# GpSimd subtracts the upper part of each output weight row block in four pieces of 256 columns, not in one of 1024

## The chip, the cores and the metric

The kernel runs on one core of a Trainium2 chip. Its time is the device time of one execution, in microseconds (us). A core has a tensor engine (PE, with its weight loads shown apart as PEld), a vector engine (VectorE, DVE in the profile), a scalar engine (ScalarE, ACT), GpSimd (POOL) and SyncE (SP), which here only issues DMAs. Each engine executes its own instructions in order; between engines there are semaphores.

## The reference, cut to what matters

One encoder layer over two sets of 512 tokens (D = 1024). The weights of interest are those of the output projection after the attention:

```python
hn = rms_norm(x, p['norm_attn'])
proj = jnp.einsum('bsd,de->bse', hn, p['w_in'])
...
oa = block_attention(qa, ka, va, 1.0 / math.sqrt(GQA_HEAD_DIM))   # 8 query heads, 2 key heads
...
ob = block_attention(qm, km, vb, 1.0 / math.sqrt(MLA_NOPE + MLA_ROPE))   # 8 heads over latents
o = jnp.concatenate([rms_norm(oa, p['out_norm_a']), rms_norm(ob, p['out_norm_b'])], axis=-1)
x = x + jnp.einsum('bse,ed->bsd', o, p['w_o'])
h2 = rms_norm(x, p['norm_ffn'])
x = x + expert_choice_moe(h2, p['w_router'], p['w_gate'], p['w_up'], p['w_down'])   # 16 experts
```

## The kernel before, in words

Matrix products of float32 are made of float32r products: each operand is split into an upper part (the value rounded to float32r) and the rest, and a product is the sum of two or three partial products. The output weights `w_o` (1024 x 1024) are split in the same way into `wo["hi"]` and `wo["lo"]`, during the attention, long before the output projection reads them.

The program goes through projection (to about 165 us), attention (to about 354 us), output projection and routing (to about 490 us), and the experts. Attention runs over 32 heads, g = 0 to 31: set 0 with its 8 GQA heads and 8 latent (MLA) heads, then set 1 likewise. Each head is four units of 128 queries. For a unit PE makes scores, VectorE takes the row maxima (`nmax`, L1471), ScalarE the exponentials (`prob`, L1403), PE turns them over (L1309), VectorE or ScalarE copies them back (`probT`), and once a head PE multiplies with the values (L1324). PE keeps three banks of scores and so runs three units ahead at most.

The order of the work is written out by hand on each engine. What touches the change:

- **GpSimd**, in each head g: the copy of the rotary keys if g starts an MLA group (`copy_rotary_keys`, L1239, for g = 24 and 25 in set 1; PE's scores of head 25 wait for the first pair), then one split of the output weights if g is in `split_at` (heads 20, 21, 22, 23, then 25, 26, 28, 29), then `add_halves(g - 2)` (L1185 and L1187), and in odd heads `scale_heads` (L1194), which multiplies two finished heads by the reciprocals of their sums.
- **A split** of row block i: `wo["hi"] = w` rounded (L1224), a wait for that, `wo["lo"] = w - wo["hi"]` (L1226), and a wait until that has ended. ScalarE has scaled the block before (L1388), one head ahead.
- **SyncE's queue**, in order: after `scale_heads(n)` it stores that pair of heads (L1136), loads two more row blocks of `w_o` (L1144, 1 MB, twice more during set 1), and loads the queries of the next two MLA heads as `q_blocks` (L1130, three DMAs for a head).
- **VectorE** turns a head's `q_blocks` over into `q_turned` (L1462), one unit before they are due. ScalarE rounds them to `qhi` (L1380), VectorE takes the rest `qlo = q_turned * gain - qhi` (L1454), a scalar_tensor_tensor with two inputs in SBUF, and PE's scores of that head wait for `qlo`. For the GQA heads the same operation reads PSUM and one tile in SBUF.

Of the kernel before, what the change touches and what calls it, by code (L numbers as in the profile page):

```python
# [13 lines left out]
F32 = mybir.dt.float32  # L14
F32R = mybir.dt.float32r
U32 = mybir.dt.uint32
ALU = mybir.AluOpType
# [7 lines left out]
SETS, SEQ, D = 2, 512, 1024  # L25
# [63 lines left out]
class Phase:  # L89
# [8 lines left out]
    def sem(self, name):  # L98
        self.sems.append(self.nc.alloc_semaphore(f"{name}_{self.suffix}"))
        return self.sems[-1]  # L100
# [912 lines left out]
def attend(phase, project_signals, a, k, att, wo, ps, banks, o_dram, r_dram, q_dram, wo_loaded):  # L1013
# [56 lines left out]
    wo_hi, wo_lo, wo_scaled = sem("wo_hi"), sem("wo_lo"), sem("wo_scaled")  # L1070
# [103 lines left out]
    def gpsimd_program(pool, row_roots, last_squares, query_roots, key_roots, row_norms, rotate_keys_pe, rotate_queries, rotate_keys, mla_parts, group_sums, acc_done):  # L1174
        LAST = T - 1

        def add_halves(g):

            n = g // 2
            rows, other = (slice(0, VD), slice(VD, P)) if g % 2 == 0 else (slice(VD, P), slice(0, VD))  # L1180
            both, head = att["ot"][g % 2][:].rearrange("d (i t) -> d i t", i=TS), att["heads"][n % OUT_RING][rows]
            pool.wait_ge(ot_copied, g + 1)
            if n >= OUT_RING:
                pool.wait_ge(o_stored[n % OUT_RING], STORED + 16 * (n // OUT_RING))
            pool.tensor_copy(head, both[other]).then_inc(o_shifted, 1)  # L1185
            pool.wait_ge(o_shifted, g + 1)
            pool.tensor_tensor(head, head, both[rows], ALU.add).then_inc(o_added, 1)  # L1187
            pool.wait_ge(o_added, g + 1)

        def scale_heads(n):  # L1190

            heads = att["heads"][n % OUT_RING]
            pool.wait_ge(r_loaded[n % 2], MLA_STORED + 32 * (n // 2 + 1))
            pool.tensor_tensor(heads, heads, att["r"][n % 2][:].rearrange("d (t i) -> d i t", i=TS), ALU.mult).then_inc(o_scaled, 1)  # L1194
            pool.wait_ge(o_scaled, n + 1)

        def finish_rows():


            row_squares, query_squares, key_squares = last_squares  # L1200
            row_squares()
            query_squares()
            pool.wait_ge(rows_ready, LAST)
            for part in mla_parts(LAST - 1):
                part()
            key_squares()
            row_roots(LAST)
            row_norms(LAST)
            rotate_keys_pe(LAST)
            rotate_queries(LAST)  # L1210
            rotate_keys(LAST)
            add_halves(0)
            query_roots(LAST)
            key_roots(LAST)
            pool.wait_ge(rk_done, T)
            add_halves(1)
            for part in mla_parts(LAST):
                part()

        def split_output_weights(pool, i):  # L1220

            raw = wo["raw"][:, i % 4, :]
            pool.wait_ge(wo_scaled, i + 1)
            pool.tensor_copy(wo["hi"][:, i, :], raw).then_inc(wo_hi, 1)  # L1224
            pool.wait_ge(wo_hi, i + 1)
            pool.tensor_tensor(wo["lo"][:, i, :], raw, wo["hi"][:, i, :].bitcast(F32), ALU.subtract).then_inc(wo_lo, 1)  # L1226

        split_at = {HEADS + 4: 0, HEADS + 5: 1, HEADS + 6: 2, HEADS + 7: 3, HEADS + QH + 1: 4, HEADS + QH + 2: 5,
                    HEADS + QH + 4: 6, HEADS + QH + 5: 7}
        copies = {QH: (2, 0, 0), QH + 1: (1, TS * QH, 2),  # L1230
                  HEADS + QH: (2, TS * (HEADS - 2), 4), HEADS + QH + 1: (1, TS * (HEADS + QH), 6)}

        def copy_rotary_keys(g):
            to, unused, count = copies[g]
            pool.wait_ge(prep_lo, prep_index["k", g // HEADS * HEADS + QH] + 1)
            if unused:
                pool.wait_ge(score_ready, unused)
            for m, part in enumerate((khi, klo)):
                pool.tensor_copy(part[to][NOPE:QK, :], part[0][NOPE:QK, :].bitcast(F32)).then_inc(pe_copied, 1)  # L1239
                pool.wait_ge(pe_copied, count + m + 1)  # L1240

        pool.wait_ge(proj_done, T)
        finish_rows()
        for g in range(GROUP, ALL):
            if g in copies:
                copy_rotary_keys(g)
            if g in split_at:
                split_output_weights(pool, split_at[g])
                pool.wait_ge(wo_lo, split_at[g] + 1)
            add_halves(g - 2)  # L1250
            if g % 2 and g > GROUP:
                scale_heads(g // 2 - 2)
        add_halves(ALL - 2)
        scale_heads(HEAD_PAIRS - 2)
        group_sums(0)
        pool.wait_ge(acc_done, 1)
        add_halves(ALL - 1)
        scale_heads(HEAD_PAIRS - 1)
# [171 lines left out]
    def vector_program(dve, row_stats, query_stats, key_stats, rb_done, rk_done, o_low, route_rest):  # L1430
# [37 lines left out]
        for u in range(NU + STEPS):  # L1468
# [30 lines left out]
            elif u == NU + 2:  # L1499
# [5 lines left out]
                      "ones_ready": ones_ready, "o_stored": o_stored, "mla_stored": project_signals["mla_stored"],  # L1505
                      "w_loaded": project_signals["w_loaded"]}
    return (sync_program, gpsimd_program, tensor_program, scalar_program, vector_program), attend_signals


# [1041 lines left out]
```

## Time and profile before

| | |
|---|---|
| median of three runs | 1035.9 us (1035.71 to 1036.63) |
| the profiled execution | 1035.18 us |
| its span, first to last instruction | 1033.4 us |
| PE busy | 1004.9 us, 97% of the span |
| VectorE busy | 850.3 us, 82% |
| ScalarE busy | 760.2 us, 74% |
| GpSimd busy | 486.2 us, 47% |
| the eight subtractions of L1226 | 19.1 us |

The shares are means over the whole program, whose stages have different limits. What matters for the change is the stretch from 270 to 340 us, where the eight splits lie, and there the order of the instructions on each engine with the idle time before them.

### The profile page before, as it was taken

The numbers are of one execution on the slowest core, as the hardware profiler recorded it, in microseconds if no ns is written. First come the engines' busy times: TensorE is split into PE (matmuls) and PEld (weight loads), VectorE is DVE, ScalarE is ACT, GpSimd is POOL, SyncE is SP. The second block draws the span as 40 slices with busy tenths as digits, with TensorE's granted clock in tenths as the row PEclk, the third lists the DMA queues.
The fourth block names the chain that finished last, engine by engine and source line by source line (L and its number), as shares of the span: only waits on it lengthen the run. The fifth ranks groups of instructions, "written<-read, shape, count | busy, mean of one in ns | idle before, by whom it ended". The sixth has DMA issues, their size and how long they took to land.

```text
span 1033.4 us, 15654 instructions
## 1 busy us (share of the span) xinstructions
PE 1004.9 (97%) x5055; PEld 806.6 (78%) x5055; DVE 850.3 (82%) x1062; ACT 760.2 (74%) x1022; POOL 486.2 (47%) x425
## 2 busy tenths in 40 slices
PE   8999999999999999995999999999999999999997
PEld 7999986666666688774888888888888888888885
DVE  6788778887888533379999999999999999999982
ACT  7665668888989745546777787778877888788772
POOL 2477679634688655446343244424442344324011
PEclk9999999999999999997999999999999999999999
DMA  9344250432443498853999999999999999999983
GB/s 330 79 116 128 79 161 12 129 72 58 129 125 71 132 254 237 232 159 142 393 398 403 398 406 411 403 400 398 420 400 402 398 419 399 403 398 408 414 330 41
DMA packets 109134, 276.02 MB, mean 267 GB/s; under 512 B 58322, under 2 KB 66733, under 8 KB 85405
## 3 DMA queue, kind: packets, MB, share of 16 engines
q1 hardware_dynamic: 103280, 258.11, 67.3%
q0 software_dynamic: 5744, 17.29, 6.7%
q8 instruction: 25, 0.41, 0.2%
q14 instruction: 25, 0.20, 0.1%
q10 hardware_dynamic: 60, 0.01, 0.0%
HBM read 247.46 MB, written 27.92 MB: 266 GB/s over the span
## 4 chain that ended last, share of the span: by engine, by line
PE 51%; DMA 1%; DVE 1%; issue 0%; ACT 0%; POOLq 0%; POOL 0%
PE ps L2223 11%; PE ps L2225 11%; PE ps L2224 11%; PE ps L2239 5%; PE ps L2237 5%; PE ps L2238 5%; PE ps L2190 1%; DMA out<-y,give 1%; DMA xt<-h,idxT 0%; DVE idx L1972 0%; DVE affT L1978 0%; DVE gates L1967 0%; POOLq L2497 0%; POOL out L2182 0%; ACT y L2351 0%
## 5 line engine op out<-in xcount | busy, mean ns | idle before, releaser
L2393 DVE TENSOR_TENSOR lo<-raw,hi 128x2048 fp32r<-128x2048 f32 x191 | 430.6, 2285 | 29.6 <-ACT hi L2315 29.3
L2315 ACT ACTIVATE hi<-raw 128x2048 fp32r<-128x2048 f32 x192 | 364.2, 1917 | 67.6 <-PE ps L2225 56.7
L2223 PE MATMUL ps<-hi,xehi 128*128 128x512 f32 x480 | 188.5, 393 | 0.1
L2225 PE MATMUL ps<-hi,xelo 128*128 128x512 f32 x480 | 187.3, 390 | 0.0
L2224 PE MATMUL ps<-lo,xehi 128*128 128x512 f32 x480 | 186.8, 389 | 0.0
L2147 POOL DMA_INDIRECT xe<-h,take x60 | 110.7, 1845 | 25.1 <-issue 13.7
L2142 POOL COPY take<-idx 128x4 uint32 (+1 forms) x15 | 31.0, 2068 | 188.6 <-DVE xt L2409 188.3
L1471 DVE TENSOR_REDUCE nmax<-ps 128x1 f32<-128x512 f32 x128 | 85.9, 680 | 28.4 <-PE ps L1300 15.1
L2225 PEld LDWEIGHTS ps<-hi,xelo 128*128 128x128 f32 x480 | 90.1, 188 | 19.0
L2223 PEld LDWEIGHTS ps<-hi,xehi 128*128 128x128 f32 x480 | 90.3, 188 | 18.6 <-issue 0.5
L2224 PEld LDWEIGHTS ps<-lo,xehi 128*128 128x128 f32 x480 | 90.2, 188 | 18.4
L1403 ACT ACTIVATE prob<-ps,nmax 128x512 f32<-128x512 f32 x128 | 87.5, 684 | 10.0 <-DVE nmax L1471 9.4
L2237 PE MATMUL ps<-hi,hthi 128*128 128x512 f32 x240 | 93.5, 390 | 0.0
L2239 PE MATMUL ps<-hi,htlo 128*128 128x512 f32 x240 | 93.5, 389 | 0.0
L2238 PE MATMUL ps<-lo,hthi 128*128 128x512 f32 x240 | 93.4, 389 | 0.0
L1309 PEld LDWEIGHTS ps<-ident,prob 128*128 128x128 f32 x512 | 63.5, 141 | 18.2 <-issue 1.2
L1309 PE MATMUL ps<-ident,prob 128*128 128x128 f32 x512 | 76.6, 272 | 0.0
L2157 POOL DMA_INDIRECT out<-y,give x15 | 24.4, 1628 | 110.3 <-ACT y L2351 87.6
L529 POOL TENSOR_TENSOR small<-small,minus_half 128x1 f32<-128x1 f32 (+4 forms) x40 | 67.3, 1682 | 3.3
L2239 PEld LDWEIGHTS ps<-hi,htlo 128*128 128x128 f32 x240 | 45.1, 188 | 9.4
L2238 PEld LDWEIGHTS ps<-lo,hthi 128*128 128x128 f32 x240 | 45.1, 188 | 9.3
L2237 PEld LDWEIGHTS ps<-hi,hthi 128*128 128x128 f32 x240 | 45.1, 188 | 9.3
(312 smaller groups left out, 2062.5 us busy)
## 6 DMA issues: line engine op xcount, KB each, us to landing
raw<-in_w_down SPq DMA_DIRECT2D x64, 1024.0 KB, 9.0
raw<-in_w_gate SPq DMA_DIRECT2D x60, 1024.0 KB, 9.4
raw<-in_w_up SPq DMA_DIRECT2D x60, 1024.0 KB, 8.9
w_raw<-in_w_in SPq DMA_DIRECT2D x8, 592.0 KB, 8.5
x<-in_x SPq DMA_DIRECT2D x8, 512.0 KB, 5.3
r<-reciprocal_sums SPq DMA_DIRECT2D x32, 128.0 KB, 3.0
attention_out<-pj SPq DMA_DIRECT2D x16, 256.0 KB, 2.3
woraw<-in_w_o SPq DMA_DIRECT2D x4, 1024.0 KB, 5.5
```

What stands on the lines that cost most here:

```text
L1309: turned = pe.transpose(ps[:, T_BANKS[u % 2], cols], att["p"][u % 3][:, cols], k["ident"][:])
L1403: act.activation(att["p"][v % 3][:], ps[:, S_BANKS[v % 3], :], ACT.Exp, bias=att["nmax"][:, v:v + 1], accum_out=att["sum"][:, v:v + 1]).th ...
L1471: dve.tensor_reduce(att["nmax"][:, u:u + 1], ps[:, S_BANKS[u % 3], :], AX.X, ALU.max, negate=True).then_inc(max_done, 1)
L2147: pool.indirect_dma_start(xe[:, q * PART:(q + 1) * PART], None, h2_quarters, bass.IndirectOffsetOnAxis(moe["take"][:, q:q + 1], 0)).then_i ...
L2223: pe.matmul(ps[:, dst[n], :], rowhi[:, c, :], hi[w][:, cols], start=c == 0, stop=False)
L2224: pe.matmul(ps[:, dst[n], :], rowhi[:, c, :], lo[w][:, cols], start=False, stop=False)
L2225: last = pe.matmul(ps[:, dst[n], :], rowlo[:, c, :], hi[w][:, cols], start=False, stop=c == KD - 1)
L2237: pe.matmul(ps[:, Y[n], :], hthi[:, f, :], hi[w][:, cols], start=f == 0, stop=False)
L2238: pe.matmul(ps[:, Y[n], :], hthi[:, f, :], lo[w][:, cols], start=False, stop=False)
L2239: last = pe.matmul(ps[:, Y[n], :], htlo[:, f, :], hi[w][:, cols], start=False, stop=f == KD - 1)
L2315: act.activation(hi[s][:], raw[r][:], ACT.Copy).then_inc(hi_done, 1)
L2393: dve.tensor_tensor(lo[s][:], raw[r][:], hi[s][:].bitcast(F32), ALU.subtract).then_inc(lo_done, 1)
```

## The change

The subtraction of L1226 is written as four, over 256 columns each. The semaphore `wo_lo` is raised by the last of the four; between them there is no wait. Tiles, values and the order of everything else are the same.

```diff
+        PIECES = 4
+
         def split_output_weights(pool, i):
 
             raw = wo["raw"][:, i % 4, :]
             pool.wait_ge(wo_scaled, i + 1)
             pool.tensor_copy(wo["hi"][:, i, :], raw).then_inc(wo_hi, 1)
             pool.wait_ge(wo_hi, i + 1)
-            pool.tensor_tensor(wo["lo"][:, i, :], raw, wo["hi"][:, i, :].bitcast(F32), ALU.subtract).then_inc(wo_lo, 1)
+            for c in range(0, D, D // PIECES):
+                cols = slice(c, c + D // PIECES)
+                last = pool.tensor_tensor(wo["lo"][:, i, cols], raw[:, cols], wo["hi"][:, i, cols].bitcast(F32), ALU.subtract)
+            last.then_inc(wo_lo, 1)
```

On GpSimd the rows of the fourth split (head 23) and what follows it, up to the rotary keys of head 24, stand in the program before like this, with the semaphores that each waits for (`ot` is the head's output from PSUM, `pj` the tile in which finished heads are gathered, `r` the reciprocals):

```order
199 L1224 CAST wohi<-woraw 128x1024 [waits wo_scaled_p,o_added_p]
200 L1226 TENSOR_TENSOR wolo<-woraw,wohi 128x1024 [waits wo_hi_p]
201 L1185 COPY pj<-ot_108 64x4x128 [waits pj_stored2_p,ot_copied_p,wo_lo_p]
202 L1187 TENSOR_TENSOR pj<-pj,ot_108 64x4x128 [waits o_shifted_p]
203 L1194 TENSOR_TENSOR pj<-pj,r_110 128x4x128 [waits mla_stored3_p,o_added_p]
204 L1239 CAST khi_96<-khi_90 32x512 [waits score_ready_p,prep_lo_p,o_scaled_p]
205 L1239 CAST klo_97<-klo_94 32x512 [waits pe_copied_p]
```

In the changed program the same place reads (its lines behind the loop are numbered five higher):

```order
202 L1226 CAST wohi<-woraw 128x1024 [waits wo_scaled_p,o_added_p]
203 L1230 TENSOR_TENSOR wolo<-woraw,wohi 128x256 [waits wo_hi_p]
204 L1230 TENSOR_TENSOR wolo<-woraw,wohi 128x256 x3
205 L1185 COPY pj<-ot_108 64x4x128 [waits pj_stored2_p,ot_copied_p,wo_lo_p]
206 L1187 TENSOR_TENSOR pj<-pj,ot_108 64x4x128 [waits o_shifted_p]
207 L1194 TENSOR_TENSOR pj<-pj,r_110 128x4x128 [waits mla_stored3_p,o_added_p]
208 L1244 CAST khi_96<-khi_90 32x512 [waits score_ready_p,prep_lo_p,o_scaled_p]
```

Nothing changes its place there; one row has become four, and only the first of them waits. The other four engines have the same instructions and waits as before. On SyncE's queue these rows follow the end of L1194 in that place (`o_scaled`), in both programs:

```order
101 L1136 DMA attention_out<-pj 128x4x128 [waits o_scaled_p]
102 L1144 DMA woraw<-in_w_o 128x2x1024 [waits wo_loaded,wo_lo_p]
103 L1130 DMA q_blocks_105<-latent_q 32x16x32 [waits q_turned_p]
104 L1130 DMA q_blocks_105<-latent_q 32x16x32 x2
105 L1130 DMA q_blocks_106<-latent_q 32x16x32 [waits q_turned_p]
106 L1130 DMA q_blocks_106<-latent_q 32x16x32 x2
```

These six DMAs of L1130 load the queries of heads 26 and 27; they stand where they stood, behind the store of the heads that GpSimd has scaled.

## Rows read from the trace of the kernel before

**Rows 1.** Busy time by engine, 269.7 to 300.6 us (us, busy us and instructions).

```profile
269.70:300.60 30.90, 29.90 (x168) 18.55 (x167) 25.30 (x40) 28.49 (x64) 29.28 (x23) 1.00 0.28 81
```

**Rows 2.** GpSimd's groups by line and shape: busy us, mean ns of one.

```profile
L1226 POOL TENSOR_TENSOR wolo<-woraw,wohi 128x1024 fp32r<-128x1024 f32 x8 | 19.1, 2384 | 0.6
L1638 POOL TENSOR_TENSOR acc<-osq 128x256 f32<-128x256 f32 x8 | 5.9, 737 | 0.6
L1676 POOL TENSOR_TENSOR otlo<-o,othi 128x512 fp32r<-128x512 f32 x2 | 2.5, 1292 | 0.0
```

**Rows 3.** Timeline of GpSimd: start us, us, instruction.

```profile
269.73 0.61 POOL L1185 COPY pj<-ot 64x512 f32<-64x512 f32 x1 [5.71 <-issue]
...
291.78 1.04 POOL L1224 CAST wohi<-woraw 128x1024 fp32r<-128x1024 f32 x1
292.89 2.37 POOL L1226 TENSOR_TENSOR wolo<-woraw,wohi 128x1024 fp32r<-128x1024 f32 x1
295.33 0.95 POOL L1185 COPY pj<-ot 64x512 f32<-64x512 f32 x1
...
297.72 1.54 POOL L1194 TENSOR_TENSOR pj<-pj,r 128x512 f32<-128x512 f32 x1
...
299.99 0.61 POOL L1239 CAST klo<-klo 32x512 fp32r<-32x512 f32 x1
301.51 0.61 POOL L1185 COPY pj<-ot 64x512 f32<-64x512 f32 x1 [0.92 <-POOL klo L1239]
...
323.62 0.72 POOL L1185 COPY pj<-ot 64x512 f32<-64x512 f32 x1 [4.07 <-issue]
```

**Rows 4.** Timeline of GpSimd, two subtractions that follow without a wait.

```profile
443.91 2.54 POOL L1676 TENSOR_TENSOR otlo<-o,othi 128x512 fp32r<-128x512 f32 x2
```

**Rows 5.** VectorE: L1454 over the program (ns min/median/max), then its timeline.

```profile
L1454 DVE SCALAR_TENSOR_TENSOR qlo<-q_turned,gcol,qhi x16: 737/804/2208, 189.6 to 340.8; 96x512 fp32r<-96x512 f32 x16
```

```profile
293.61 2.21 DVE L1454 SCALAR_TENSOR_TENSOR qlo<-q_turned,gcol,qhi 96x512 fp32r<-96x512 f32 x1
...
301.65 1.02 DVE L1454 SCALAR_TENSOR_TENSOR qlo<-q_turned,gcol,qhi 96x512 fp32r<-96x512 f32 x1
...
307.28 0.71 DVE L1462 STREAM_TRANSPOSE q_turned<-q_blocks 96x512 f32<-96x512 f32 x1
```

**Rows 6.** Timeline of PE: start us, us, instruction, [idle before it, releaser].

```profile
295.87 0.63 PE L1280 MATMUL ps<-ident,kv_rows 128*64 128x128 f32 x4 [0.93 <-DVE qlo L1454]
...
303.31 0.48 PE L1298 MATMUL ps<-khi,qhi 96*128 96x512 f32 x1
...
309.46 0.50 PE L1298 MATMUL ps<-khi,qhi 96*128 96x512 f32 x1 [0.43 <-ACT prob L1403]
```

**Rows 7.** SyncE's queue, 255 to 345 us: waits (us, times, longest us), then timeline.

```profile
SPq L1136 <- POOL pj L1194: 32.8, 7, 8.2
```

```profile
299.29 0.36 SPq L1136 DMA_DIRECT2D attention_out<-pj  x1
299.75 0.45 SPq L1144 DMA_DIRECT2D woraw<-in_w_o  x1
...
301.57 1.32 SPq L1130 DMA_DIRECT2D q_blocks<-latent_q  x2
```

**Rows 8.** DMA issues, 300.2 to 301.6 us: KB, us to landing (median; min/median/max).

```profile
woraw<-in_w_o SPq DMA_DIRECT2D x1, 1024.0 KB, 5.7
q_blocks<-latent_q SPq DMA_DIRECT2D x3, 64.0 KB, 5.3
```

```profile
DMA to landing us min/median/max: 5.2/5.3/5.5
```

**Rows 9.** Timeline of ScalarE.

```profile
308.02 0.72 ACT L1380 ACTIVATE qhi<-q_turned,gcol 96x512 fp32r<-96x512 f32 x1 [0.33 <-DVE q_turned L1462]
308.65 0.66 ACT L1403 ACTIVATE prob<-ps,nmax 128x512 f32<-128x512 f32 x1
```

**Rows 10.** Timelines of GpSimd and VectorE at the last split.

```profile
334.47 2.39 POOL L1226 TENSOR_TENSOR wolo<-woraw,wohi 128x1024 fp32r<-128x1024 f32 x1
```

```profile
336.82 0.74 DVE L1454 SCALAR_TENSOR_TENSOR qlo<-q_turned,gcol,qhi 96x512 fp32r<-96x512 f32 x1
```

## The prediction

> **What bounds the kernel now.** I began with busy time by stretch. Over the whole span GpSimd is less than half busy, but from 269.7 to 300.6 us, where the first four splits lie, it works 29.28 of 30.90 us [rows 1], and its timeline there shows rows that follow each other at 0.07 us, with no idle time given, from 269.73 us until the one at 301.51 [rows 3]. In this stretch GpSimd is late for everything, and whatever is added to it pushes all that follows. PE is busy 29.90 us of the same stretch. It sets the pace, and a wait on its row is time of the kernel.
>
> Next I looked for who waits for the subtraction. On VectorE the same `qlo` operation is there 16 times; the quickest takes 0.737 us, the longest 2.208 [rows 5]. The longest starts at 293.61, in the middle of GpSimd's subtraction (292.89 to 295.26), and ends at 295.82, 0.56 us after it. The one at 301.65 starts inside a GpSimd copy (301.51 to 302.12), and ends at 302.67, 0.55 after it. So a VectorE operation with two inputs in SBUF waits until GpSimd's running instruction has ended, and then needs 0.56 us. PE shows what the long one costs: 0.93 us idle at 295.87, released by `qlo` [rows 6]. Of the eight subtractions only this one is met by such an operation, since the GQA heads' operations read PSUM.
>
> Last I looked at who waits for GpSimd itself. SyncE's queue stands up to 8.2 us at L1136 for the scaled heads. It goes on at 299.29, 0.03 after L1194 has ended (297.72 + 1.54 = 299.26), and only then issues 1 MB of `w_o` and the queries of heads 26 and 27 [rows 3, 7]. The third DMA of head 26 is issued at 301.57 and lands 5.2 us later, at 306.77 [rows 7, 8]. VectorE reads those queries at 307.28 [rows 5]: **the slack is 0.51 us**. Behind that read there is none. ScalarE waits for `q_turned` before `qhi` at 308.02, then makes the next exponentials at 308.65 [rows 9], and PE, idle for 0.43 us, waits for those at 309.46 [rows 6].
>
> **What the change removes: the long wait.** If the other things stayed, the `qlo` of head 24 would wait for a piece, not for the whole. But GpSimd is late by then (below, 0.43 us a split, three splits: 1.29), so it is the rounding of the fourth block that lies there, from 291.78 + 1.29 = 293.07 to 294.11. `qlo` then ends at 294.11 + 0.56 = 294.67, before PE is free (295.87 - 0.93 = 294.94). PE's wait goes: -0.93 us at that point, whether the pieces let VectorE in or not.
>
> **What it adds: fixed cost per instruction.** No row has this subtraction over 256 columns. The nearest is an addition over 256 columns, 0.737 us [rows 2]. Two subtractions of 512 columns that follow without a wait take 2.54 us together, where each is given 1.292, so the second starts 0.044 before the first has ended [rows 2, 4]. Four pieces: 4 x 0.737 - 3 x 0.044 = 2.82 us, against 2.384: **+0.43 us a split**. Bounds: nothing at all, if the fixed part were hidden behind the piece before; and, with the 0.07 us that stands between waiting instructions, 4 x 0.737 + 3 x 0.07 = 3.16, +0.77. I take 0.43, since the row that follows without a wait is the nearest in kind.
>
> The Trainium skill, "Perfetto Trace Analysis", section "GPSIMD Engine Instruction", holds that GpSimd's reported spans do not add up, and that one should go by the spacing of the starts. The trace agrees, by a little: 2.54 us for 2 x 1.292. By plain durations the split would cost 0.56 more, and the sum below would come to +1.75 in place of +1.22.
>
> **Where the added time goes.** Four splits before L1194 make 4 x 0.43 = 1.73 us (head 24's `qlo` costs GpSimd some 0.34 us now, as the 0.95 us of the copy at 295.33 against 0.61 show, and will cost about that in the other place). Three things could become late.
> - ScalarE's copy of a head's output waits for the sum of two heads before; GpSimd may be a whole head late there (295.33 to 301.51, some 6 us, by its copies [rows 3]). Nothing.
> - PE's scores of head 25 (303.31) need the rotary keys, which are ready at 299.99 + 0.61 = 300.60. That becomes 302.33, against 303.31 - 0.93 = 302.38 once PE is ahead. On the edge, at worst some 0.3 us of a gain that is lost a little later anyway.
> - The queries of head 26. All of SyncE's rows behind L1136 move by 1.73, and the landing with them: 306.77 + 1.73 = 308.50. VectorE, which would come there at 307.28 or up to 0.93 earlier, stands still until then. Its read is **1.22 us later than now**, and behind it are the maxima of a unit, `qhi`, the exponentials and PE.
>
> So the 0.93 us gained are handed back, and 1.22 more: they don't add, since the landing hangs on GpSimd and SyncE alone. After that GpSimd has idle time (0.92 us before the row at 301.51, 4.07 before that at 323.62 [rows 3]) and is no longer late; the 0.43 us of the later four splits go into that. From here on every engine follows PE, and nothing that I see gives time back before the output projection. **Sum: 1.73 - 0.51 = +1.22 us** on the profiled execution, 1035.18 to 1036.4. That execution lay 0.7 us below the median of the three runs; on the median the sum gives 1037.1 us.
>
> **The rivals.**
> - *The gain stays.* If a split cost less than 0.13 us more (4 x 0.13 = 0.51), the landing stays hidden, and PE keeps up to 0.93: 1035.0 us on the median. For it: the wait of 2.21 us is real. Against it: every row of short GpSimd instructions has a fixed part (0.737 us for a quarter of the columns is far above a quarter of 2.384). The Trainium skill, "SBUF — State Buffer", section "Who interferes with whom", says the port shared by the two engines is held for a whole instruction, which speaks for shorter instructions; the 2.21 us agree. Chance 0.12.
> - *The pieces are dearer.* At the upper bound, +0.77 a split, the queries come 3.1 us later than now, and the sum is 3.1 - 0.51 = +2.6: 1038.5 us. It passes 0.2% (2.07 us) from 0.65 us a split on. For it: no row shows four such instructions in a row; against it: the two of L1676. Chance 0.14.
> - *The port is not given up between pieces.* GpSimd then holds VectorE for all four. At the first collision that changes nothing (the rounding lies there). At the last split it does: its pieces would run from 334.47 + 1.22 + 0.43 = 336.12 to 338.94, and head 30's `qlo` comes at 336.82 + 1.22 = 338.04 [rows 10]; it would end at 338.94 + 0.56 = 339.50 and not at 338.8. +0.7 on top, 1037.8 us. The Trainium skill, "GPSIMD Engine Reference", section "Instruction dispatch", says that a core of GpSimd starts the next instruction as soon as its own share is done, which would leave no gap. No row here shows two GpSimd instructions without a wait under such a VectorE operation. Chance 0.08.
>
> **How the numbers follow.** The forecast has 0.66. 0.2% of the time, 2.1 us, is about what a measurement of this kernel tells from no change. Forecast and gain both lie within it; beyond it lie most of the dearer pieces (0.12), and a little of the forecast and of the third rival, if the medians differ by half a microsecond as the three runs do (0.07). Faster by more would need over twice the 0.93 us: 0.04. Slower 0.19, the same 0.77. The range goes from the gain's 1035.0 to the dear pieces' 1038.5.
>
> **What would show it.** The pieces' starts 0.69 us apart, and no idle time on GpSimd from 270 to some 302 us. No `qlo` over 1.3 us near 294, and no idle PE there. L1136 going on near 301.0, the third query DMA of head 26 landing near 308.5, and VectorE idle for 1 to 2 us in front of its turn. The prediction is wrong if that turn isn't waited for, if its wait is made good by 345 us, or if a new long `qlo` appears elsewhere.

## The result, and the profile after

The changed kernel takes 1038.39 us (median of 12 runs, 1036.99 to 1040.05) against 1035.8 us for the kernel before: a ratio of 1.0025, 95% interval 1.0017 to 1.0032, so 2.6 us slower. The forecast was +1.2 us, 1037.1 us on the median, with a range from 1035.0 to 1038.5. The profiled execution took 1038.74 us, with a span of 1036.9 us. Two runs of the experiments, one of e2 with 4823.24 us and one of e4 with 2596.89 us, lie far from all others and are left out below.

Everything up to the first split is 0.70 us later in this profile than in that of before (GpSimd's copy at 270.43 and not at 269.73, [rows 3]), which differs from execution to execution. Times in two profiles are therefore compared from that copy on.

GpSimd's timeline after; the lines of the first four splits answer to [rows 3]:

```profile
270.43 0.61 POOL L1185 COPY pj<-ot 64x512 f32<-64x512 f32 x1 [5.71 <-issue]
...
275.22 2.81 POOL L1230 TENSOR_TENSOR wolo<-woraw,wohi 128x256 fp32r<-128x256 f32 x4
...
293.77 1.04 POOL L1226 CAST wohi<-woraw 128x1024 fp32r<-128x1024 f32 x1
294.88 3.13 POOL L1230 TENSOR_TENSOR wolo<-woraw,wohi 128x256 fp32r<-128x256 f32 x4
...
300.11 1.55 POOL L1194 TENSOR_TENSOR pj<-pj,r 128x512 f32<-128x512 f32 x1
301.73 0.95 POOL L1244 CAST khi<-khi 32x512 fp32r<-32x512 f32 x1
302.75 0.61 POOL L1244 CAST klo<-klo 32x512 fp32r<-32x512 f32 x1
```

Four pieces take 2.81 us together. The fourth split has 0.32 us more, because VectorE goes ahead of its first piece. L1194 starts 300.11 - 270.43 = 29.68 us after the copy; before it was 297.72 - 269.73 = 27.99. GpSimd is 1.69 us late.

VectorE's timeline after, at the operations of [rows 5]; in brackets the idle time before one and who ended it:

```profile
294.32 1.03 DVE L1459 SCALAR_TENSOR_TENSOR qlo<-q_turned,gcol,qhi 96x512 fp32r<-96x512 f32 x1
...
308.99 0.71 DVE L1467 STREAM_TRANSPOSE q_turned<-q_blocks 96x512 f32<-96x512 f32 x1 [2.18 <-DMA q_blocks<-latent_q]
...
324.11 0.71 DVE L1467 STREAM_TRANSPOSE q_turned<-q_blocks 96x512 f32<-96x512 f32 x1
```

The 2.21 us operation now takes 1.03, and ends 0.54 after the rounding that it met (293.77 + 1.04 = 294.81). Later VectorE stands 2.18 us for the queries of head 26, where it did not wait before. The last line is its turn of head 28, which in the kernel before is this one:

```profile
320.89 0.71 DVE L1462 STREAM_TRANSPOSE q_turned<-q_blocks 96x512 f32<-96x512 f32 x1
```

SyncE's queue after, then how long the three query loads of head 26 were under way (they answer to [rows 7, 8]):

```profile
301.69 0.37 SPq L1136 DMA_DIRECT2D attention_out<-pj  x1
302.15 0.45 SPq L1144 DMA_DIRECT2D woraw<-in_w_o  x1
302.65 5.35 SPq L1130 DMA_DIRECT2D q_blocks<-latent_q  x6
...
303.98 0.67 SPq L1130 DMA_DIRECT2D q_blocks<-latent_q  x1
```

```profile
DMA to landing us min/median/max: 5.0/5.2/5.4
```

The third is issued at 303.98 and lands 5.0 us later; VectorE starts at 308.99. PE after, at the places of [rows 6], the idle time in brackets:

```profile
303.50 0.47 PE L1303 MATMUL ps<-khi,qhi 96*128 96x512 f32 x1 [0.36 <-POOL klo L1244]
...
311.17 0.50 PE L1303 MATMUL ps<-khi,qhi 96*128 96x512 f32 x1 [1.94 <-ACT prob L1408]
311.50 0.54 PE L1304 MATMUL ps<-klo,qhi 96*128 96x512 f32 x1
311.84 0.63 PE L1305 MATMUL ps<-khi,qlo 96*128 96x512 f32 x1
```

PE's stop for the exponentials has grown from 0.43 to 1.94 us. And there is something that the prediction has not got: the matmuls behind it take 0.54 and 0.63 us, where such ones took 0.40. The windows by stretch say why; the last three columns are PE's granted clock, DMA share and GB/s:

```profile
309.00:311.00 2.00, 0.23 (x3) 0.00 (x0) 1.97 (x4) 1.27 (x3) 1.68 (x3) 1.00 0.25 27
311.00:312.00 1.00, 0.83 (x3) 0.69 (x4) 1.00 (x3) 1.00 (x4) 0.28 (x1) 0.80 0.00 0
312.00:313.00 1.00, 1.00 (x7) 0.80 (x5) 0.77 (x2) 1.00 (x4) 0.92 (x2) 0.50 0.10 37
...
314.00:315.00 1.00, 1.00 (x5) 0.80 (x4) 1.00 (x3) 0.75 (x2) 1.00 (x1) 0.50 0.09 31
315.00:316.00 1.00, 1.00 (x7) 0.40 (x7) 0.88 (x2) 1.00 (x4) 0.94 (x2) 1.00 0.00 0
```

After its stop PE runs at half its clock, the lower of the two levels, until 315 us.

**Where the 2.5 us are.** From GpSimd's copy to the turn of head 26 it was 307.28 - 269.73 = 37.55 us, and is 308.99 - 270.43 = 38.56: +1.01. From there to the turn of head 28 it was 320.89 - 307.28 = 13.61, and is 324.11 - 308.99 = 15.12: +1.51. Together 2.52, with 2.59 measured between the medians. What follows is nearly as long as before: to the end of the span 712.5 us before, 712.8 after. (The two profiled spans differ by 3.5 us: the 0.70 us ahead of the copy, these 2.52, and 0.28 behind.)

### The profile page after: what moved, and what is told of

Its sections match the earlier page's. It is cut to its first block, busy times and chain, and to the rows that moved or that the text cites. A ratio compares the mean times of both kernels' runs of the same rounds, so it can differ in the third digit from the quotient of the medians.

```text
span 1036.9 us, 15678 instructions
## 1 busy us (share of the span) xinstructions
PE 1007.2 (97%) x5055; PEld 808.1 (78%) x5055; DVE 851.6 (82%) x1062; ACT 760.7 (73%) x1022; POOL 490.3 (47%) x449
## 4 chain that ended last, share of the span: by engine, by line
PE 52%; DVE 1%; DMA 1%; issue 0%; ACT 0%; POOLq 0%; POOL 0%
PE ps L2228 11%; PE ps L2230 11%; PE ps L2229 11%; PE ps L2244 5%; PE ps L2242 5%; PE ps L2243 5%; PE ps L2195 1%; DMA out<-y,give 1%; PE ps L2294 1%; DVE idx L1977 0%; DVE affT L1983 0%; DVE gates L1972 0%; POOLq L2502 0%; POOL out L2187 0%; ACT y L2356 0%
```

## The experiments

These two distances are a measure that each profile gives, of one execution of its kernel, and it keeps the two parts of the loss apart. For all experiments (us; the medians against the kernel before on the same chip, with the interval of the ratio):

| kernel | median, before | ratio, 95% | copy to head 26 | head 26 to 28 |
|---|---|---|---|---|
| before | | | 37.55 | 13.61 |
| changed | 1038.39, 1035.8 | 1.0025 (1.0017 to 1.0032) | 38.56 | 15.12 |
| e1 first four in pieces | 1038.0, 1035.71 | 1.0019 (1.0010 to 1.0027) | 39.19 | 15.21 |
| e2 last four in pieces | 1035.62, 1035.71 | 1.0000 (0.9991 to 1.0009) | 37.62 | 13.62 |
| e3 queries ahead | 1034.53, 1035.71 | 0.9989 (0.9980 to 0.9998) | 36.49 | 13.61 |
| e4 same time, no pieces | 1037.48, 1035.71 | 1.0020 (1.0011 to 1.0028) | 38.88 | 13.61 |
| e5 PE kept busy | 1037.92, 1036.02 | 1.0016 (1.0007 to 1.0025) | 38.55 | 13.60 |
| e6 two pieces | 1037.07, 1036.02 | 1.0007 (0.9998 to 1.0016) | 38.55 | 15.13 |
| e7 whole, queries ahead | 1035.96, 1036.02 | 0.9999 (0.9990 to 1.0008) | 37.58 | 13.60 |
| e8 same time, queries ahead | 1035.47, 1036.02 | 0.9994 (0.9985 to 1.0003) | 36.47 | 14.27 |
| e9 w_o behind the queries | 1034.8, 1035.89 | 0.9991 (0.9982 to 1.0000) | 36.40 | 13.61 |
| e10 one split in pieces | 1035.66, 1035.89 | 1.0000 (0.9991 to 1.0009) | 37.55 | 13.59 |
| e11 two splits, queries ahead | 1034.73, 1035.89 | 0.9990 (0.9981 to 0.9999) | 36.61 | 13.59 |
| e12 changed again | 1038.27, 1035.89 | 1.0023 (1.0011 to 1.0034) | 38.45 | 15.11 |

**e1 and e2: which splits cost.** Pieces in the first four splits alone (e1, below), or in the last four alone (e2, the same with `i >= 4`):

```diff
+            pieces = PIECES if i < 4 else 1
+            for c in range(0, D, D // pieces):
```

> Only the first four splits (heads 20 to 23) are in four pieces, the last four whole. Theory (GpSimd's added time, 4 x 0.43 us, makes the queries of head 26 land late, VectorE stands, PE stops for 1.9 us, and the granted clock of PE falls to 0.50 for some 3 us): the whole loss stays, +2.6 us against before, with VectorE idle 2.2 us before its turn of head 26 and PEclk 0.5 in the 3 us behind PE's stop. Rival (every split in pieces costs, wherever it stands, by VectorE's operations that collide with GpSimd): half of it, +1.3 us.

> Only the last four splits (heads 25, 26, 28, 29) are in four pieces. Theory (lateness before the queries of head 26): no loss, within 0.5 us of before, with the 2.2 us operation at head 24 and its 0.9 us of PE idle as before. Rival (each split in pieces costs): +1.3 us.

e1 is 2.3 us slower, e2 not at all, and e2 has its 2.25 us operation and PE's wait of 0.97 us at head 24 as the kernel before. The loss belongs to the splits that lie ahead of the queries of head 26. In e1's profile VectorE waits 2.75 us there; the last of the three query loads took 5.5 us to land and not 5.0.

**e3: the queries out of GpSimd's shadow.** The three loads are left out at their old place (not shown) and stand here:

```diff
+            if n == HEADS // 2 + 2:
+                load_queries(HEADS + QH + 2)
             if n:
                 store_heads(n - 1)
```

> The changed kernel with all eight splits in pieces, and in SyncE's queue the three loads of head 26's queries stand ahead of the store of the heads that GpSimd has scaled, not behind it. Theory: the queries land before 300 us, VectorE doesn't wait for them, PE doesn't stop, its clock stays, and the gain at head 24 is left less the wait for the rotary keys: 0.93 - 0.36 = 0.6 us faster than before (between 0.9 faster and equal). Rival (the rotary keys, or the pieces themselves, cost the time): still slower than before, +1 to +2.6 us.

With all eight splits in pieces and these three DMAs ahead of the store, the kernel is 1.2 us faster than the kernel before, more than the 0.6 expected; the interval reaches from 0.2 to 2.1. VectorE doesn't wait for the queries, and PE's only idle time near them is 0.39 us for the rotary keys. So neither the pieces nor the keys carry the loss.

**e4: the same time on GpSimd, without pieces.** Whole subtractions, and 80 columns done once more:

```diff
+            if i < 4:
+                pool.tensor_tensor(wo["lo"][:, i, 0:80], raw[:, 0:80], wo["hi"][:, i, 0:80].bitcast(F32), ALU.subtract).then_inc(extra, 1)
+                pool.wait_ge(extra, i + 1)
```

> The kernel before with whole subtractions; in each of the first four splits GpSimd subtracts the first 80 columns once more ahead of the whole, and waits for that: some 0.42 us a split (0.35 us for 80 columns by the rows of 64 and 128, and 0.07 for the wait), as much as the pieces cost. Theory (only the time on GpSimd matters): as the changed kernel, +2.0 to +2.8 us, with the same late queries. Rival (it is the pieces, how they share the port with VectorE): at most +0.5 us.

1.8 us slower by the median and 2.1 by the ratio, at the lower end of what was expected, with a like wait for the queries (2.43 us). Time on GpSimd in that place is enough. The profiled execution is one whose clock holds (the third number from the end) although PE stood for 2.21 us; it took 1037.12 us, 0.36 less than the median.

```profile
309.00:312.00 3.00, 0.88 (x4) 0.68 (x5) 2.97 (x5) 2.32 (x5) 1.30 (x2) 1.00 0.09 7
312.00:316.00 4.00, 4.00 (x22) 2.20 (x21) 3.39 (x6) 4.00 (x10) 3.78 (x4) 1.00 0.20 72
```

**e5: PE kept busy while it waits.**

```diff
+            if u == TS * (HEADS + QH + 2) - 1:
+                for _ in range(16):
+                    pe.transpose(ps[:, R_BANK, 0:P], k["ident"][:], k["ident"][:])
             if u >= 3:
                 pe.wait_ge(exp_done, u - 2)
```

> The changed kernel, with 16 transposes of the identity into a bank of PSUM that is not in use, on PE ahead of the scores at which it stops for 1.9 us (head 25, unit 3); they are extra work that nothing reads, some 1.4 us by the 0.09 us of the rows of four transposes. The late queries stay, so VectorE's wait of 2.2 us stays too. Theory (the loss of 2.5 us is 1.0 us of waiting and 1.5 us of slow matmuls after it, because PE stood idle): PEclk stays 1.00 from 309 to 316 us and the loss falls to about 1.0 us, 1036.7 us. Rival (the loss is the wait alone, and the clock's fall costs nothing since PE isn't the limit there): still +2.3 to +2.6 us.

The profile is as expected: the transposes fill 1.91 us, PE waits 0.16 us, the clock stays at 1.00, and from head 26 to 28 it is 13.60 us. Timeline of PE and the window behind it:

```profile
309.04 1.91 PE L1294 MATMUL ps<-ident 128*128 128x128 f32 x16
311.11 0.50 PE L1306 MATMUL ps<-khi,qhi 96*128 96x512 f32 x1 [0.16 <-ACT prob L1411]
```

```profile
312.00:316.00 4.00, 4.00 (x22) 2.20 (x21) 3.38 (x6) 4.00 (x10) 3.78 (x4) 1.00 0.27 68
```

The time is not: 1.9 us over the kernel before, neither the 1.0 expected nor the rival's 2.3 to 2.6. The profiled execution took 1036.98 us, the median is 0.9 above it.

The mean granted clock of every single run tells more. It lies between 0.988 and 0.992, and is 0.988 in 10 of the 12 runs of the changed kernel, 5 of 11 of e4, 3 of 11 of e6, 2 of 11 of e1 and 2 of 7 of e12; in none of e5, and in none of 97 runs of the kernel before. All runs with 0.988 took 1037.9 us or more. In e4, where both kinds are frequent, the five took 1038.5 us in the median and the six others 1037.0: the 1.5 us of the profiles again. (A run can have the fall and a higher mean, as the profiled one of e1 with 0.990, so these are the least counts.) But two runs of e5 took 1037.92 us at a mean of 0.992, the highest of any run here, so late without a fall (an estimate: a fall of 1.5 us in 1036 takes some 0.0015 off the mean). So the step from +1.0 to +2.5 is the slow clock in the profiles, and the fall is the rule in the changed kernel; what else makes e5's median 1.9 us, and so how much of the changed kernel's median is the clock alone, is not settled.

**e6: two pieces of 512 columns.**

```diff
-        PIECES = 4
+        PIECES = 2
```

> All eight splits in two pieces of 512 columns: 2 x 1.292 - 0.044 = 2.54 us, 0.16 us more than whole, so GpSimd is 0.62 us late before the queries of head 26. Theory: the queries land 0.1 us after the time at which VectorE reads them now; VectorE waits for about 1 us, since it comes earlier, the time is that of before within 0.4 us if PE's clock holds, and 1.0 to 1.5 us over it in runs where the clock falls. The long operation at head 24 then meets the first of the two pieces and ends 0.56 us behind it, some 1.5 us long and not 2.8. Rival (VectorE gets the port only when both pieces have ended): that operation takes over 2.5 us. Rival (a split in pieces costs its pieces): +1 us and more.

A split costs 0.15 us more (2.53 by the rows of 2.52 and 2.54), as expected. The median is 1.1 us over, with an interval that reaches just past no change, and runs from 1035.26 to 1038.93 us; five of the eleven are below 1036.4, five above 1037.9. In the profiled one, which is among the longer ones (1038.27 us), the three query loads land 5.4, 5.6 and 6.0 us after their issue (minimum, median, maximum), and the clock falls. That with so little lateness the landing time decides, which differs between executions, fits this but is not shown: one execution was profiled. The operation at head 24 speaks against the rival with the port; GpSimd, then VectorE:

```profile
293.52 1.28 POOL L1230 TENSOR_TENSOR wolo<-woraw,wohi 128x512 fp32r<-128x512 f32 x1
...
294.76 1.73 POOL L1230 TENSOR_TENSOR wolo<-woraw,wohi 128x512 fp32r<-128x512 f32 x1
```

```profile
293.75 1.60 DVE L1459 SCALAR_TENSOR_TENSOR qlo<-q_turned,gcol,qhi 96x512 fp32r<-96x512 f32 x1
```

It comes in the first piece, ends 0.55 us after it (295.35 against 294.80), and the second piece takes 0.44 us longer. VectorE gets in between two instructions that have no wait between them.

**e7 and e8: is it the order of the queue, or the lateness?** The kernel before with head 26's queries ahead (e7), and e4 with them ahead (e8), the edits as above.

> The kernel before, whole subtractions, with the three query loads of head 26 ahead of the store in SyncE's queue. Theory: the order of the queue alone brings nothing where the queries were in time, since the 2.2 us operation at head 24 stays: within 0.4 us of before. Rival (the gain of 1.2 us with the queries ahead came from the new order of the queue, not from what happens at head 24): 1.0 to 1.2 us faster than before.

> The kernel before with whole subtractions, the 80 columns subtracted once more in each of the first four splits (GpSimd as late as with the pieces), and the query loads of head 26 ahead of the store. Theory (what takes VectorE's long wait away is that GpSimd is late, so that it meets the rounding and no longer the subtraction; pieces are not needed): 0.6 to 1.2 us faster than before, as with pieces and the queries ahead, with an operation of about 1.1 us at head 24. Rival (the pieces give the gain): not faster than before.

e7 is as fast as the kernel before, and the distance from copy to head 26 is the same within 0.03 us; the new order alone brings nothing. e8 is 0.55 us faster, and its interval reaches just past no change. At head 24 it does what e3 does (1.09 us). At head 26 a difference shows between whole subtractions and pieces, since GpSimd is late and meets VectorE there too. GpSimd and VectorE in e8:

```profile
307.43 2.39 POOL L1233 TENSOR_TENSOR wolo<-woraw,wohi 128x1024 fp32r<-128x1024 f32 x1
```

```profile
308.40 1.97 DVE L1461 SCALAR_TENSOR_TENSOR qlo<-q_turned,gcol,qhi 96x512 fp32r<-96x512 f32 x1
```

In e3 the same operation meets the pieces and takes 1.00 us. That is the distance from head 26 to 28 in the table, 14.27 us in e8 against 13.61. The two gains are 0.63 us apart, which agrees, but their intervals are wider than that. The theory was right at head 24 and too narrow: a late GpSimd needs the pieces elsewhere.

**e9: the 1 MB load behind the queries.** The queries stay behind the store, and `load_output_weights(3)` goes behind them.

```diff
             if first % HEADS > QH or n == HEADS // 2 - 2:
                 load_queries(first)
                 load_queries(first + 1)
+            if n == HEADS // 2 + 3:
+                load_output_weights(3)
```

> The changed kernel; on SyncE's queue the last load of w_o (1 MB) stands behind the six query loads of heads 26 and 27, which stay behind the store that waits for GpSimd. The queries are issued some 1.2 us later than in the kernel before, and no longer share the DMA engines with that load: some 2.7 us to landing and not 5.0 to 6.0. Theory (late is only what is issued late and also lands behind 1 MB): they land about 36 us after GpSimd's copy at 270 us, before VectorE comes (36.5); no wait, 0.6 to 1.2 us faster than before. Rival (the late issue alone is enough): VectorE still waits, +1 us or more.

1.1 us faster than the kernel before, with an interval that ends at no change; the loss in any case is gone. The three loads take 2.8 us in the median and not 5.2, and that is enough: late issue alone does no harm.

**e10: only the split that VectorE meets.**

```diff
+            pieces = PIECES if i in (3,) else 1
```

> Only the fourth split (head 23, the one that VectorE met) is in four pieces, order of the queue as before. GpSimd is 0.43 us late before the store, and some 0.3 more where VectorE goes between the pieces. Theory: the wait at head 24 goes (operation under 1.3 us, no PE idle there), but the queries of head 26 land about when VectorE reads them now, so that it waits for them, up to 1 us; the time is that of before within 0.5 us in runs where PE's clock holds, and about 1 us over it in the others. Rival (with the lateness gone the gain stays): 0.7 us or more faster.

The operation at head 24 takes 0.74 us, so it doesn't wait at all, and comes away with the whole gain. VectorE then stands 1.41 us for the queries, more than the 1 us expected, and the turn of head 26 is 37.55 us after the copy, to the hundredth what it is in the kernel before; the time is the same. PE stands for 1.53 us in this profile, and its clock holds.

**e11: pieces where VectorE is met, and the queries ahead.** The splits of heads 23 and 25 in pieces, with e3's edit.

> Pieces only in the splits that VectorE can meet (head 23 and head 25), the first three whole, and head 26's query loads ahead of the store. Theory: no long operation at head 24, no late rotary keys (0.4 us of PE idle in the run with all in pieces), no late queries: 1.0 to 1.5 us faster than before, the fastest of all. Rival (the first three splits in pieces matter too, or the rotary keys' wait is hidden anyway): no better than 1.2 us.

1.2 us faster than the kernel before, as e3 and e9; the three can't be told apart. The wait for the rotary keys is gone, but PE then waits 0.41 us for the exponentials at the next place. The rival holds: that wait was hidden, for the distance from copy to head 26 is no shorter here (36.61 us) than in e3 (36.49).

**e12: the changed kernel again.**

> The changed kernel once more, beside the others on one chip, for a second profile of it. Theory: +2.0 to +2.8 us, VectorE's turn of head 26 about 1.0 to 1.6 us later than in the kernel before, counted from GpSimd's copy at 270 us; if PEclk falls behind it, head 28 is another 1.5 us later, and if not, no more. Rival (the loss arises elsewhere): the turn of head 28 is not later than that of head 26.

+2.4 us; head 26 is +0.90 and head 28 another 1.50 later, with the clock down again.

## Why the prediction was right about the wait and short in its size

- **The cost of a split** was put at +0.43 us (2.82 in all); it is 2.81. The pieces start 0.69 to 0.70 us apart (338.11, 338.81, 339.51, 340.20 in the last split). Right.
- **The operation at head 24** meets the rounding, takes about 1.0 us, and PE's 0.93 us are gone. Right; e8 shows that it needs no pieces for that, e10 that the pieces would do it too, without any lateness.
- **The rotary keys**: 0.36 us of PE idle, where at worst 0.3 was expected. The sum had left out that VectorE's operation of head 25 now falls on the copy of the keys, which takes 0.95 us (301.73) and not 0.60. Hidden, as e11 shows.
- **The queries of head 26** were to be read 1.22 us later; it was 1.01, and 0.90 in e12. They were issued 1.70 us later and took 5.0 us to land, not 5.2. e3 and e9 take this wait away in two ways, and the loss goes with it; e4 brings it about without pieces. This is shown. The gain of 1.1 to 1.2 us that is left in e3 and e9 is barely clear of no change: the intervals end at 0.9998 and 1.0000.
- **"From here on every engine follows PE, and nothing that I see gives time back"**: here the sum failed. It took for granted that PE, once it goes on, is as fast as before. In four profiles (the changed kernel, e1, e6, e12) the granted clock fell to 0.50 behind stops of PE of 1.8 to 2.5 us, and head 26 to 28 was longer by 1.50 to 1.60; in that of e4, with a stop of 2.21 us, it held. By the profile the missing term is +1.51: with it the sum would have been 1.22 + 1.51 = +2.7, against 2.52 in the profile and 2.6 between the medians. That the medians agree so well proves less, since e5 is late without a fall too. In the same stretch lies a new long `qlo`, which the prediction had named as a sign of being wrong: 1.51 us at 315.45, head 27. It doesn't make the loss: in e1 and e12 that operation takes 0.75 us, and the stretch is as long.
- **The rivals.** The gain did not stay (e7 and e10 show on what it hangs). The dearer pieces had about the right time, 1038.5 us, by a wrong mechanism; that the measured 1038.39 us lies inside the range, whose upper end they set, is luck. The port is given up between pieces: in the last split of the changed kernel an operation starts at 340.04, the third piece ends about 340.25 (its start, 339.51, and the 0.74 of such a piece), and the operation ends at 340.79, as one that had not waited. It need not be the next gap: in e11 an operation that starts at 294.37, 0.07 us before the first piece ends, ends at 295.67, 0.54 us after the end of the second (294.40 + 0.73 = 295.13). In no run did such an operation wait for all pieces.
- **The chances.** 0.77 stood on a change within 0.2%; measured is 0.25%, its interval from 0.17 to 0.32%. In the profile the missing term moved it there.

Open: what decides whether the clock falls. PE stood 2.21 us in e4 and the clock held, 1.83 us in e12 and it fell, so the length of the stop doesn't decide alone. Open too: what makes runs of e5 late without a fall.

## What to carry to other kernels

A late engine is to be followed through the queues: here 1.7 us on GpSimd, in a place that nobody on PE's path waits for, reached PE through a store in SyncE's queue, because loads that depend on nothing of it stood behind that store and behind 1 MB more. Put such loads ahead of the wait; then the pieces gained some 1.2 us here (0.2 to 2.1 by the interval). And where PE is made to stand, its stop is not the whole price: look at the granted clock of the microseconds behind it.

## What the runs showed of the hardware

- A VectorE operation with two inputs in SBUF gets the port between two GpSimd instructions even where no wait stands between these, and ends 0.54 to 0.56 us after the one that held it (the changed kernel, e6, e11); the next GpSimd instruction then takes 0.3 to 0.55 us longer (0.32 in the changed kernel, 0.44 in e6, 0.55 in e10). An operation of e11 that started 0.07 us before such a gap missed it; that of e10, 0.10 us before one, did not. The Trainium skill, "SBUF — State Buffer", section "Who interferes with whom", has the port held for a whole instruction, with which all of these rows agree.
- The granted clock fell to 0.50 behind a stop of PE of 1.83 us (e12), and head 26 to 28 took 1.5 us longer; 16 transposes that nothing reads, in that gap, kept it at 1.00 in the profile taken (e5). It held behind a stop of 2.21 us in e4 and one of 1.53 in e10.
- Loads of 64 KB behind a load of 1 MB in one queue took 5.0 to 6.0 us to land (the changed kernel and e6), and 2.6 to 3.0 without it (e9).
